# Moving the split-weight buffers of an fp32 two-block kernel by 64, 256 and 320 bytes

## The reference, cut to what matters

```python
def first_block(x, mem, ...):
    mem_n = rms_norm(mem, mem_norm_g)
    h = x
    for layer in range(2):
        xn = rms_norm(h, norm_mix_g[layer])
        # layer 0: gated linear attention and RWKV-7; layer 1: RG-LRU and mLSTM
        h = h + mixed @ w_mix_out[layer]
        h = h + memory_cross_attention(rms_norm(h, norm_xattn_g[layer]), mem_n, wq, wkv, wo)
        h = h + conv_glu_ffn(rms_norm(h, norm_ffn_g[layer]), w_up, conv_w, conv_b, w_down)
    return rms_norm(h, final_norm_g)

def second_block(x, ...):
    for l in range(2):
        h = rmsnorm(x, norm_mix[l])
        # layer 0: spatial gating and latent attention; layer 1: retention
        x = x + mix
        h = rmsnorm(x, norm_ffn[l])
        x = x + (silu(h @ w_gate) * (h @ w_up)) @ w_down
```

## Time and profile before

| what | us |
|---|---|
| median of 3 runs | 3118.99 |
| lowest and highest | 3117.21, 3120.8 |
| span of the profiled execution, first to last instruction | 3114.6 |
| PE busy | 3014.8 (97%) |
| PEld busy | 2468.0 (79%) |
| DVE busy | 1737.4 (56%) |
| ACT busy | 1273.3 (41%) |
| POOL busy | 319.5 (10%) |

### The profile page before, as it was taken

The page is one execution under the profiler, slowest core; times in us unless marked ns, Lnnn a source line. Parts: engine busy times, 40 slices in busy tenths (PEclk is TensorE's granted clock), DMA queues, the critical chain, the costliest instruction groups (busy, mean ns, idle before and its releaser), DMA issues.

```text
span 3114.6 us, 41482 instructions
## 1 busy us (share of the span) xinstructions
PE 3014.8 (97%) x17696; PEld 2468.0 (79%) x17696; DVE 1737.4 (56%) x2154; ACT 1273.3 (41%) x1702; POOL 319.5 (10%) x285
## 2 busy tenths in 40 slices
PE   8988889999999999999999998999999999999999
PEld 6876678778888766778887775689998888878998
DVE  6445454647544775546543745676666453566665
ACT  5433343434322564433322545543444333344442
POOL 1010001000000100000000200124310000013340
PEclk9999999999999999999999999999999999999999
DMA  5341023223332311323332330133332222233331
GB/s 185 112 112 29 29 73 126 98 75 92 101 88 79 115 54 54 108 68 95 97 91 87 93 88 27 55 95 99 109 105 92 85 88 95 69 87 102 103 105 65
DMA packets 340104, 274.89 MB, mean 88 GB/s; under 512 B 28768, under 2 KB 308832, under 8 KB 339408
## 3 DMA queue, kind: packets, MB, share of 16 engines
q1 hardware_dynamic: 335552, 252.83, 27.2%
q0 software_dynamic: 4368, 19.41, 1.8%
HBM read 263.83 MB, written 8.39 MB: 87 GB/s over the span
## 4 chain that ended last, share of the span: by engine, by line
PE 87%; DVE 6%; ACT 5%; issue 2%; POOL 0%; DMA 0%; DVEq 0%; SPq 0%; ACTq 0%; POOLq 0%
PE ps L189 86%; ACT arena L203 2%; DVE arena L212 1%; ACT whi L206 1%; DVE arena L220 1%; DVE wlo L212 1%; PE ps L192 1%; DVE hT L212 1%; ACT L203 0%; DVE sml L229 0%; POOL arena L212 0%; ACT arena L206 0%; DVE xlo L220 0%; DVE split L212 0%; DVE arena L223 0%
## 5 line engine op out<-in xcount | busy, mean ns | idle before, releaser
L189 PE MATMUL ps<-split,whi 128*128 128x512 f32 (+1 forms) x3008 | 900.7, 377 | 14.0 <-DVE split L212 6.1
L212 DVE TENSOR_TENSOR wlo<-wraw,whi 128x2048 fp32r<-128x2048 f32 (+5 forms) x261 | 562.4, 2157 | 491.2 <-ACT whi L206 490.9
L189 PE MATMUL ps<-xhi,whi 128*128 128x512 f32 (+2 forms) x2040 | 764.2, 380 | 16.5 <-DVE xlo L212 7.0
L189 PE MATMUL ps<-xhi,wlo 128*128 128x512 f32 (+2 forms) x1984 | 742.0, 374 | 0.0
L189 PE MATMUL ps<-xlo,whi 128*128 128x512 f32 (+2 forms) x1944 | 729.9, 376 | 0.0
L189 PEld LDWEIGHTS ps<-split,whi 128*128 128x128 f32 x3008 | 548.7, 188 | 142.3 <-issue 24.5
L206 ACT ACTIVATE whi<-wraw 128x2048 fp32r<-128x2048 f32 (+5 forms) x261 | 457.2, 1755 | 349.7 <-PE ps L189 245.5
L189 PE MATMUL ps<-split,wlo 128*128 128x512 f32 (+1 forms) x1504 | 559.6, 372 | 0.0
L189 PEld LDWEIGHTS ps<-xhi,whi 128*128 128x128 f32 (+1 forms) x2040 | 380.6, 188 | 100.1 <-issue 14.6
L189 PEld LDWEIGHTS ps<-xhi,wlo 128*128 128x128 f32 (+1 forms) x1984 | 373.6, 188 | 69.6 <-issue 5.1
L189 PEld LDWEIGHTS ps<-xlo,whi 128*128 128x128 f32 (+1 forms) x1944 | 365.9, 188 | 68.2
(11 more groups left out here) (132 smaller groups left out, 2430.9 us busy)
## 6 DMA issues: line engine op xcount, KB each, us to landing
wraw<-in_ffn_w_up SPq DMA_DIRECT2D x128, 512.0 KB, 5.2
wraw<-in_odd_w_in SPq DMA_DIRECT2D x24, 1024.0 KB, 5.1
wraw<-in_ffn_w_gate SPq DMA_DIRECT2D x44, 512.0 KB, 4.0
wraw<-in_ffn_w_down SPq DMA_DIRECT2D x20, 1024.0 KB, 5.1
wraw<-in_ffn_w_down SPq DMA_DIRECT2D x24, 768.0 KB, 4.4
wraw<-in_xattn_wkv SPq DMA_DIRECT2D x16, 1024.0 KB, 5.6
wraw<-in_xattn_wq SPq DMA_DIRECT2D x8, 1024.0 KB, 5.3
wraw<-in_xattn_wo SPq DMA_DIRECT2D x8, 1024.0 KB, 5.2
```

What stands on the lines that cost most here:

```text
L189: return self.e.matmul(out, lhsT, rhs, start=start, stop=stop, skip_group_check=True)
L212: return self.e.tensor_tensor(out, a, b, op)
```

## The change

The two lists of buffers are declared one by one, with unused tensors between them. The 16 columns of apart0 are 64 bytes, the 48 of apart1 are 192, the 16 of apart2 are 64. So whi0 stays, whi1 is 64 bytes further, wlo0 256 bytes, wlo1 320 bytes, and everything declared behind them (ident, ones, par, sml and the arena with its other view, split) is 320 bytes further. All of it still fits.

```diff
-        whi = [sbr(f"whi{i}", WSLOT) for i in range(NSPL)]
-        wlo = [sbr(f"wlo{i}", WSLOT) for i in range(NSPL)]
+        whi, wlo = [sbr("whi0", WSLOT)], []
+        sb("apart0", 16)
+        whi.append(sbr("whi1", WSLOT))
+        sb("apart1", 48)
+        wlo.append(sbr("wlo0", WSLOT))
+        sb("apart2", 16)
+        wlo.append(sbr("wlo1", WSLOT))
```

## The result

The changed kernel takes 3127.64 us in the median of 6 runs (3123.23 to 3129.45), the kernel before 3118.14 in 6 runs on the same chip (3115.41 to 3120.8). The ratio is 1.0028, 95% interval 1.0017 to 1.0039: slower by some 9 us, where +14.7 was forecast. The profiled execution spans 3126.2 us, 11.6 more than before.

The account below looks back on a forecast made before the run. TensorE, busy 97% of the span, was taken as the bound: number of matmuls times their pace. +12.8 + 6.4 - 4.5 = +14.7 us on 3114.6, plus 4.4 carried over to the median, gave 3134 us, range 3102 to 3145.

Parts of the forecast that it names:

- The cover: Making the weight halves on VectorE and ScalarE: any growth stays hidden by 245.5 us of slack at whi, 0 us.
- Odd units: 512-column matmuls with whi1, wlo1 and xhi, xlo or weights moving: the beat is lost, 2724 x 4.7 ns = +12.8 us.
- the beat: Even pace of 226.6 ns in 512-column matmul streams with equal placement, against 230.0 to 233.3 ns without it.
- Even units: Same matmuls with whi0 and wlo0: one load in three at distance 256, middle between 0 and 12.8 taken, +6.4 us.
- the settling: Start of a TensorE stream behind a wait: some ten matmuls at 232 ns each before the stream reaches 226.6.
- Arena: 3456 matmuls of 512 columns with the arena moving: pace from 233.3 to 232.0 ns, -4.5 us.
- Matmuls of 256 columns: Some 3,700 matmuls of 256 columns: placement makes no clear difference, 0 us, bounds +-4 us.
- A: Rival on the 512-column streams: even units lose the beat too and the arena's pace stays, about 3142 us; chance 0.22.
- B: Rival on the arena's streams: distances 128 and 192 allow a beat, gain up to 23.2 us; chance 0.27.
- C: Rival: paces come from something other than distance, or gains and losses cancel, 3113 to 3125 us; chance 0.18.
- The rule of the Trainium skill on two independent read ports: On TensorE: loading the next weights takes no read bandwidth from the running matmul, so no placement could matter, sum 0.

Follow-up runs that it names:

- e1: Against the kernel before, only whi1 and wlo1, with the arena and what is declared behind the buffers, stand 64 bytes further: 3129.03 us, ratio 1.0034.
- e3: Against the kernel before, only the arena is moved, 128 bytes, to distance 0 against all four buffers: 3101.98 us, ratio 0.995.
- e4: Against the kernel before, everything from hT on stands 64 bytes further, with all distances between tensors kept: 3120.27 us, ratio 1.0004.
- the sweep: Four placements of buffers and arena against the kernel before, ident, ones, par and sml declared ahead of xhi: 3130.94, 3137.48, 3136.64 and 3129.52 us.
- e2_lo256: Against the kernel before, wlo0 and wlo1 stand 256 bytes further, the arena moving along, whi0 and whi1 staying: 3119.22 us, ratio 1.0001.
- e5_lo128: Against the kernel before, wlo0 and wlo1 stand 128 bytes further, the arena moving along, whi0 and whi1 staying: 3130.97 us, ratio 1.0044.
- s3_160_192: Third placement of the sweep, against the kernel before: even buffers at 160, odd at 192, arena at 352 bytes: 3136.64 us, ratio 1.006.
- e6_arena0_norm: As e3, with the norm's tiles starting 2052 instead of 2051 columns before the arena's end: 3100.26 us, ratio 0.9941 against the kernel before.

## Why the prediction was right, and where not

*Mechanism.* Shown: the change acts through TensorE's pace alone, the pace follows the distance between moving and stationary operand (e1, e3, e4, the sweep), other engines' rows stay as they were. Why equal places allow an even pace is open: no run shows where the time goes. The cover held: ScalarE's wait for TensorE at whi is 247.7 us after, 245.5 in the earlier trace rows:

```profile
ACT whi L206 <- PE ps L189: 247.7, 41, 9.6
```

*Odd units, +12.8.* Right in kind and nearly in size: +14.3 measured. The pace without the beat was 233.3 ns there, the upper of the two ends, rather than 232.0.

*Even units, +6.4.* The step that failed, for a wrong premise: "of the three loads in a triple two (whi0) still stand at distance 0, one (wlo0) at 256". Distance 256 is distance 0, as e2_lo256 shows, so that nothing of these units changed, and one of the two ends, nothing, was the truth: +1.4 us measured. What is left of it is the settling of the earlier trace rows: each even unit now starts behind an odd one and has to find its beat again, 10.91 us instead of 10.88. In the changed kernel's unit that starts at 783.80 the first 7 matmuls take 1.62 us, 231 ns each, and the other 41 take 9.29 us, 226.6 ns each:

```profile
783.80 0.39 PE L189 MATMUL ps<-xhi,whi 128*128 128x512 f32 x1
...
785.42 0.39 PE L189 MATMUL ps<-xhi,wlo 128*128 128x512 f32 x1
...
794.71 0.40 PE L189 MATMUL ps<-xhi,whi 128*128 128x512 f32 x1
```

The rows had no two distances a multiple of 256 apart, yet 512 was only the grain in which I had tabled the places; nothing showed it as the period.

*Had the case been what I took it for*, e5_lo128 shows its price, 3.8 ns per matmul for one load in three, above the middle of 2.35 that I had taken.

*Arena, -4.5.* Mis-sized: -0.6. The arena's mean before was 232.9 ns, not the 233.3 of the one stretch read, and it is 232.7 after. I had taken the 232.0 ns of a stream that is settling for the pace of any stream without a beat. A settling stream is not a sample of an unsettled one: at 192 it is 233.2, at 128 232.4. Nor is the 230.0 of the earlier trace rows what I called it: by the tiles' addresses only two of each three moving operands there stand 48 bytes further, the third 12, which is not a multiple of 16, though the prediction says that no row tests a shift inside a line. Over the ten traces the matmuls at 432 (176 within 256) have a mean of 231.1 ns.

*Matmuls of 256 columns, 0.* Mis-sized: -4.1, at the edge of the +-4 allowed. The mean durations of the groups that I read for it, 282 to 286 ns, mix starts behind waits with streams; the starts would have told more (119.4 ns for xhi and xlo at 0, 118.7 for the arena at 128, 122.7 for it 4 bytes beyond), but not the gain, since no 256-column stream stood at 192 before.

*Sum.* +14.7 forecast; +14.3 + 1.4 - 0.6 - 4.1 + 0.4 = +11.4 in the profiled executions and about 9 in the medians. That the total came near is in part luck: terms too high by 9.1 us in all met terms too low by 5.8. Term by term: even units 5.0 too high, 256 columns 4.1 too high, arena 3.9 too low, odd units 1.5 too low, and 0.4 that no term had: -9.1 + 5.8 = -3.3.

*Rivals of the prediction.* A (all beats lost) is refuted for this change by the even units. B (the arena finds a beat) is refuted at the change's distances, 128 and 192, and realised at 0 by e3_arena0: the gain of 23.2 us that it named was there, only not at this placement; 18.8 of it came. C (no change, placement doesn't matter) is refuted by e1 and e3. The rule of the Trainium skill on two independent read ports ("TensorE: Matmul & The Clock Gate", section "Step-by-step: what each phase is for"), from which the prediction derived a sum of 0, does not carry to the last 3%: same shapes, same order, 226.7 or 233.3 ns by placement alone. Whether the read ports are where the operands meet, no run shows.

## What to carry to other kernels

Where TensorE streams without waits, compare the distances between starts of equal matmuls at different places of the program; if they differ with the same clock, look at where moving and stationary operand lie. For 512-column matmuls with a fresh 128-column load each, put all operands at one place within 256 bytes: 32 unused columns in front of the arena gave 16 us of 3118. And test a supposed period before building on it: one shift by half of the 512 bytes, as in e2_lo256, would have told here.

## What the runs showed of the hardware that was not expected

- The even pace of 226.67 ns is a lock. Behind a wait a stream at distance 0 takes much the same distances each time, ... 235, 233, 236, 224, 231, 236, 228, 233, 231 ns (in full 10 times in the kernel before, the last six 31 times), and then 226.67 until something interrupts (the longest stretch before has 421 matmuls). Streams at other distances run in cycles: 229.0 and 237.7 in turn for the arena before; a cycle of seven, 232, 228, 230, 233, 241, 232, 231, in other stretches of it; 226, 229, 232 at distance 64 in s3_160_192. The pace and the cycles' sums are multiples of 6.67 ns: 34, 70, 244 and 103 times.
- In the kernel before, the starts of all 53 locked stretches of 12 or more fall on the same remainder of 6.67 ns, but for a slow drift of 4 ns over the whole trace, and whatever idle time lies between. I read this as a lock to something that runs on its own. What it is, no run here shows.
- At 256 columns distance 0 locks at 120.0 ns, 18 times 6.67. Distance 192 locks too, and at a better pace: 113.33 ns, 17 times 6.67, in stretches of some 20 matmuls of the changed kernel. A kernel made of such matmuls alone would want another placement; that was not tried.
- A moving operand 4 bytes off distance 0 costs 1.9 ns at 256 columns: the same matmuls have 121.9 ns in e3_arena0 and 120.0 in e6_arena0_norm.
